# Modulation's sums over the partitions: blockwise transposes and run sums on VectorE, one constant 16-column product on TensorE, in place of four one-column products

## The reference, cut to what matters

```python
cond_act = jax.nn.silu(c)
ada = (cond_act @ w_ada + b_ada)[:, None, :]           # 1024 -> 6144, layers 0 and 1
sh1, sc1, g1, sh2, sc2, g2 = jnp.split(ada, 6, axis=-1)
u = layer_norm(x) * (1 + sc1) + sh1
...
x = layer_norm(ALPHA * x + g1 * mixed) * ln1_g + ln1_b
# layers 2 and 3: the same with silu(c) @ mod_w[i] + mod_b[i], and with silu(c_ctx) for the context
```

## Time and profile before

| what | value |
|---|---|
| median of 3 runs | 2518.83 us (2517.06 to 2518.84) |
| the profiled execution's own time | 2518.36 us |
| its span in the trace | 2516.3 us |
| busy: TensorE matmuls, weight loads, VectorE, ScalarE, GpSimd | 94%, 56%, 37%, 14%, 1% |
| mean granted TensorE clock | 0.984 of full |
| steps 0 to 3 of the modulation | until about 57 us |
| steps 4 to 51: VectorE, TensorE | about 120 to 1035 us, 161 to 1103 us |
| the two mixtures | about 1360 to 1830 us, 2050 to 2516 us |

### The profile page before, as it was taken

The page is one execution under the profiler, slowest core; times in us unless marked ns, Lnnn a source line. Parts: engine busy times, 40 slices in busy tenths (PEclk is TensorE's granted clock), DMA queues, the critical chain, the costliest instruction groups (busy, mean ns, idle before and its releaser), DMA issues.

```text
span 2516.3 us, 26389 instructions
## 1 busy us (share of the span) xinstructions
PE 2358.8 (94%) x10608; PEld 1407.4 (56%) x10608; DVE 925.1 (37%) x1976; ACT 353.5 (14%) x717; POOL 31.5 (1%) x54
## 2 busy tenths in 40 slices
PE   6999999999899999999998999988889989988986
PEld 5878698458678697457654333333377543333332
DVE  5244544544544455122754111111145531111113
ACT  1211111001120110011342111111100021111111
POOL 0100000001000000000000000000000000000000
PEclk9999999999899999999998999999989989999999
DMA  8644878756247688632035999999874359999996
GB/s 306 251 162 166 318 252 281 289 178 227 84 173 288 225 301 286 232 134 84 1 144 225 409 428 428 428 428 429 364 257 176 116 227 429 429 428 429 429 429 272
DMA packets 160899, 700.91 MB, mean 279 GB/s; under 512 B 6064, under 2 KB 15536, under 8 KB 135216
## 3 DMA queue, kind: packets, MB, share of 16 engines
q1 hardware_dynamic: 158512, 691.36, 69.9%
q0 software_dynamic: 2304, 8.39, 0.9%
HBM read 694.48 MB, written 5.24 MB: 278 GB/s over the span
## 4 chain that ended last, share of the span: by engine, by line
PE 74%; DMA 19%; DVE 3%; ACT 2%; issue 1%; SPq 1%; DVEq 0%; ACTq 0%
PE banks L614 72%; DMA ring<-in_exp_w_down_dram 19%; DMA ring<-in_w_ada_dram 1%; ACT UT L1408 1%; PE banks L751 0%; DVE acc L1751 0%; PE banks L683 0%; ACT arena L1615 0%; SPq L2574 0%; DVE X L1856 0%; DVE arena L2206 0%; DVE arena L2199 0%; PE banks L1157 0%; SPq L2648 0%; PE banks L998 0%
## 5 line engine op out<-in xcount | busy, mean ns | idle before, releaser
L614 PE MATMUL banks<-ring,arena 128*64 128x512 f32 (+2 forms) x3776 | 976.2, 593 | 77.6 <-DVE arena L2206 29.2
L614 PE MATMUL banks<-UT,ring 128*128 128x256 f32 (+1 forms) x3568 | 726.4, 362 | 6.0 <-ACT UT L1408 3.0
L614 PEld LDWEIGHTS banks<-ring,arena 128*64 128x64 f32 (+1 forms) x3776 | 360.6, 147 | 657.3 <-issue 617.3
L614 PEld LDWEIGHTS banks<-UT,ring 128*128 128x128 f32 x3568 | 617.4, 192 | 89.8 <-issue 15.4
L1778 DVE SCALAR_TENSOR_TENSOR acc<-ring,cact,acc 128x512 f32<-128x512 f32 x280 | 212.7, 760 | 9.9
L2198 DVE TENSOR_TENSOR arena<-arena,banks 128x512 f32<-128x512 f32 x32 | 34.0, 1063 | 441.1 <-PE banks L614 441.1
L1588 ACT ACTIVATE arena<-banks 128x512 f32<-128x512 f32 (+1 forms) x96 | 65.2, 679 | 798.4 <-PE banks L614 759.3
L614 PE MATMUL banks<-arena 64*128 64x512 f32 (+5 forms) x768 | 151.1, 442 | 5.0 <-ACT arena L1455 2.8
L614 PEld LDWEIGHTS banks<-arena 64*128 64x128 f32 (+2 forms) x768 | 73.5, 175 | 83.7 <-issue 68.8
L2206 DVE TENSOR_TENSOR arena<-banks,acc 128x512 f32<-128x512 f32 x32 | 22.1, 692 | 208.6 <-PE banks L614 208.6
L614 PE MATMUL banks<-ring,XN 128*128 128x512 f32 (+1 forms) x192 | 72.9, 539 | 0.0
(11 more groups left out here) (242 smaller groups left out, 1378.7 us busy)
## 6 DMA issues: line engine op xcount, KB each, us to landing
ring<-in_exp_w_gate_dram SPq DMA_DIRECT2D x64, 2048.0 KB, 22.1
ring<-in_exp_w_up_dram SPq DMA_DIRECT2D x64, 2048.0 KB, 25.2
ring<-in_exp_w_down_dram SPq DMA_DIRECT2D x64, 2048.0 KB, 17.1
ring<-in_w_in_dram SPq DMA_DIRECT2D x26, 2048.0 KB, 14.1
ring<-in_mod_w_dram SPq DMA_DIRECT2D x24, 2048.0 KB, 8.1
ring<-in_w_ada_dram SPq DMA_DIRECT2D x20, 2048.0 KB, 8.5
ring<-in_w_up_dram SPq DMA_DIRECT2D x16, 2048.0 KB, 8.2
ring<-in_w_down_dram SPq DMA_DIRECT2D x16, 2048.0 KB, 7.9
```

Source lines behind the costliest of these rows:

```text
L614: return nc.tensor.matmul(o, lhs, rhs, start=start, stop=stop)
```

## The change

A constant `fold` (128x128, one where row and column agree modulo 32) joins the constants, and a tile `folded` (128 x 2 x 16) the buffers. For steps 4 to 51, VectorE sums all chunks into `acc[:, 0]`, transposes that in 32x32 blocks into `acc[:, 1]`, and sums runs of 32 columns, which gives 128x16 partial sums. TensorE does one product: `fold` stationary, the 16 columns moving. It adds the four groups of 32 partitions and leaves the totals in each group. The eviction is four instructions on 32 partitions each.

```diff
-     ("cos2", 256), ("sin2", 256), ("zt", 256), ("tri", 128), ("iota", 64), ("low4", 16)])
+     ("cos2", 256), ("sin2", 256), ("zt", 256), ("tri", 128), ("iota", 64), ("low4", 16), ("fold", 128)])
...
+    put("fold", (np.arange(P)[:, None] % 32) == (np.arange(P)[None, :] % 32))
...
+        folded = sb("folded", [P, 2, 16])
...
                     bank = take(pe, g, None if turning else n % 2)
                     pe.wait_ge(acc_ready, n + 1)
-                    own = quarters(acc[:, n % 2, :]) if L >= 2 and 6 <= j < 10 else \
-                        acc[:, n % 2, :].rearrange("p (q c) -> p q c", c=P)
-                    for q in range(4):
-                        x = mm(bank[:, q:q + 1], own[:, q, :], C("ones", 0, 1), True, True)
-                    finish(x, g)
+                    finish(mm(bank[:, 0:16], C("fold"), folded[:, n % 2, :], True, True), g)
...
-                    emptied(V.scalar_tensor_tensor(out=dst, in0=filled(dve, g)[:, 0:4], scalar=one,
-                                                   in1=S(f"bada{L}", 4 * j, 4), op0=ALU.add, op1=ALU.add), g)
+                    own = filled(dve, g)[:, 0:16].rearrange("p (q b) -> p b q", b=4)
+                    for b in range(4):
+                        r = slice(32 * b, 32 * b + 32)
+                        x = V.scalar_tensor_tensor(out=dst[r, :], in0=own[r, b, :], scalar=one,
+                                                   in1=S(f"bada{L}", 4 * j, 4)[r, :], op0=ALU.add, op1=ALU.add)
+                    emptied(x, g)
                     evicted_steps[0] = n + 1
+
+            def mod_fold(n):
+
+                L, j, _ = MOD_STEPS[n]
+                own = quarters(acc[:, 0, :]) if L >= 2 and 6 <= j < 10 else acc[:, 0, :]
+                link(V.transpose(acc[:, 1, :], own))
+                V.tensor_reduce(folded[:, n % 2, :], acc[:, 1, :].rearrange("p (b r) -> p b r", r=32), AX.X, ALU.add)\
+                    .then_inc(acc_ready, 1)
...
-                dst = acc[:, n % 2, :]
+                dst = acc[:, 0, :]
                 link(V.tensor_scalar(dst, w[:, 0, :], cact[:, c0:c0 + 1], None, ALU.mult))
                 for k in range(1, KC):
-                    x = V.scalar_tensor_tensor(out=dst, in0=w[:, k, :], scalar=cact[:, c0 + k:c0 + k + 1],
-                                               in1=dst, op0=ALU.mult, op1=ALU.add)
-                    if k < KC - 1:
-                        link(x)
-                x.then_inc(acc_ready, 1)
+                    link(V.scalar_tensor_tensor(out=dst, in0=w[:, k, :], scalar=cact[:, c0 + k:c0 + k + 1],
+                                                in1=dst, op0=ALU.mult, op1=ALU.add))
+                mod_fold(n)
```

More of the change, by code:

```diff
@@ L1797, in mod_part @@
                                                    in1=dst, op0=ALU.mult, op1=ALU.add)
[L1798 to L1801, removed]
+                    link(x)
+                if part == 3:
+                    mod_fold(n)
             def beside(*key, flush=None):
```

## The result

The changed kernel takes 2495.31 us in the median of four runs (2494.77 to 2496.76), the kernel before 2518.63: a ratio of 0.9911 (95% interval 0.9899 to 0.9923), 23.3 us faster. The forecast was 2491.5 us, 27.3 faster. The profiled execution is the slowest of the four, 2496.76 us with a span of 2494.7.

The account below looks back on a forecast made before the run. The prediction took TensorE's matmul stream to bound the kernel in steps 4 to 51. Gains of 29.3 us less losses of 1.1 + 0.85 = 1.95 gave net 27.3 us, a median of 2491.5 us, range 2485 to 2500.

Parts of the forecast that it names:

- What bounds the kernel: TensorE's stream is the path through steps 4 to 51; later DMA paces the mixtures, which should move forward as a block.
- ordinary sum: A step's sum on TensorE without strided columns: each saves 0.60 us, 30 of them 18.0 us.
- The new product: TensorE's one product of two records per step: 0.22 us, bounds 0.20 and 0.40.
- The fold: VectorE's added transpose and run sum, 0.69 us each, with two links: 1.44 us a step.
- strided steps: Steps whose quarters take every fourth column: each saves 1.45 us on TensorE, seven counted, 10.2 us.
- The cover: VectorE's added 1.65 us a step hides in slack of at least 6.7 us, save at two steps (12 and 40).
- The evictions: On VectorE, four instructions for one: three more at about 0.07 us each, 0.21 us a step.
- steps 10 and 38: Gate's product waits for VectorE's evictions: no gain, eight instructions for two cost 0.42 us each, 0.85 us in all.
- 22 and 50: Steps where the gate's product waits for sum and eviction: 0.39 us gained each, 0.8 us.
- step 30: Before layer 1's attention, folds and evictions use 3.3 of 4.4 us of VectorE's idle time; 0.3 us gained.
- The clock: Rival: new waits at steps 12, 40, 10 and 38 each set off a clock fall costing up to 8.5 us; 2525.5, chance 0.03.
- steps 11, 12, 39 and 40: TensorE's sum waits for VectorE's fold, and the saving of the step ahead is lost: 1.1 us worse in all.

Follow-up runs that it names:

- e3: The kernel before, with transpose and run sum added on VectorE, their result unused, TensorE still taking its four products; 2521.25 us (1.0017).
- e4: The changed kernel with every block transpose done twice, one after the other; median 2503.96 us.
- e1: The kernel before, with each eviction of a sum split into four instructions of one column on all 128 partitions; 2521.82 us (1.0011).
- e2: The kernel before, with each eviction split into four instructions of 32 partitions and four adjacent columns each; 2522.53 us (1.0018).
- f1: The changed kernel with the sums of steps 9, 10, 37 and 38 in the common rotation of banks; 2488.78 us (0.9881).
- h1: The changed kernel run again, without any edit; 2495.67 us (0.9913).
- g1: The kernel before with three reorderings: gate sums' banks, sums of steps 12 and 40 one piece later, step 31 behind VectorE's chain; 2502.34 us (0.9938).

## Why the prediction was right, and where its sizes were off

**What bounds the kernel: right.** Every ordinary sum gained the same 0.66 to 0.67 us. The mixtures moved forward as a block, but for two waits of about 0.5 us.

**The new product: 0.15 us where I took 0.22**, below my lower bound of 0.20. The router's rows give the pace of products that follow each other; a pair between wide products costs less. Worth 2.6 us more over 37 sums.

**The fold: 1.46 us measured, 1.44 forecast.** The float32 transpose of 128x512 takes 0.71 us, about what the copy takes, and with the run sum and their links 1.46; in the eight strided steps it takes 1.1 us, under cover. The estimate of 1.24 us from the Trainium skill (VectorE: DVE Perf Modes, "The three transpose paths") was too high for this form; the measurement decides.

**The cover: right for this change.** e3 shows the two places and no other. It has little to spare in attention, as the two waits of e4 show, and e4's median is not accounted for.

**The evictions: the step that failed in size.** "Three more cost about 0.07 us each" took the distance of two instructions that both start at partition 0 for that of four that start at different ones. Measured 0.17 (e1, e2). An eviction takes 0.51 us more and not 0.21, and VectorE's next instruction, which used to start 0.07 us behind it, starts 0.70 us behind, 0.63 us later; at the gates, eight in a row, it is 1.15 in place of 0.42. It accounts for 1.5 us at steps 10 and 38, 0.5 at 22 and 50, and a part of step 30, where I had counted 3.3 of 4.4 us as used. Two folds and two evictions use 2 x (1.46 + 0.63) = 4.2, and the sums come 1.3 us earlier, so that VectorE and no longer TensorE is last, by about 1.1 us; the third eviction, ahead of the chain, adds its 0.63. Together about 1.8 us; TensorE's wait grew by 2.05, from 9.49 to 11.54. In the earlier trace rows VectorE waits 4.38 us before it evicts step 30. In the changed kernel the sum starts at 628.00 us, and the eviction comes without a wait:

```profile
629.63 0.67 DVE L1740 SCALAR_TENSOR_TENSOR modc<-banks,small 32x4 f32<-32x4 f32 x4
```

**The clock: a rival that came true in part.** I gave it 0.03 for four falls of 8.5 us. There were two, of 3.4 us each at the lower level, and they cost 3.2 us; f1, which takes the waits away, has neither. The sign was never in doubt. The argument against it leant on a window of 330 to 480 us, which does not hold the 0.89 us wait at 285.4 us, though the clock was at its upper level there too.

**How much of the match is luck.** The cheaper product gives about 2.5 us more than forecast, and the evictions and steps 11, 12, 39 and 40 take 3.8: errors of opposite sign leave 26.0 us for 27.3. The clock, with the two waits in the mixtures, adds the rest in the profiled run, which is 5.7 us above the forecast for it. The median is only 3.8 us above. h1's profiled run, with the same waits and both falls, takes 2491.48 us, because it has less lower clock elsewhere; that it hits the forecast is chance.

## What to carry to other kernels

The cost of a small instruction is its distance to its neighbour, and that depends on the neighbour: look for a row with the same partitions on both sides before you multiply. When work moves from the engine that bounds to one with room, list the places where the bounding engine comes upon the other's result with little to spare; here three reorderings of a few lines each removed the large waits and were worth nearly as much again as the change (21.6 against 23.3 us). Such a reordering may also pay without the change, so try it on both.

## What the runs showed that I had not expected

- Eight small VectorE instructions on 128 partitions take 0.61 us, eight on groups of 32 partitions with changing start 1.37 us. On 64 partitions, a pair with the same start stands 0.07 us apart at a duration of 0.14, and a pair with changing start 0.30 at 0.29.
- A VectorE transpose of 128x512 in float32 takes 0.71 us with a dense source and 1.10 to 1.12 us with a source of stride four.
- TensorE's clock fell from 2.4 to 1.2 GHz for 3.4 us behind a wait of 1.28 us in e1 and not behind one of 2.04 us in e2, and in g1 for 3.4 us with no wait ahead of it, behind 3.7 us of products on 64 and on 4 partitions. A kernel with several such waits spreads more from run to run: 2491.5 to 2496.9 us in the changed kernel, 2516.0 to 2519.6 in the kernel before.
